# Delta-rule norms by a product with ones, a logarithm and an exponential, in place of column sums, roots and broadcasts

## What is computed

```python
def l2norm(x):
    return x * lax.rsqrt(jnp.sum(x * x, axis=-1, keepdims=True) + EPS)

q = l2norm(q.reshape(B, T, DN_HEADS, DN_DK)) * (DN_DK ** -0.5)
k = l2norm(k.reshape(B, T, DN_HEADS, DN_DK))
...
o, S = gated_delta_rule(q, k, v, g, beta, S0.astype(f32))
```

## Time and profile before

| | |
|---|---|
| median of 3 runs | 2141.03 us (2140.2 to 2142.7) |
| the profiled execution, its own time | 2148.23 us |
| its span | 2146.4 us |
| busy: TensorE (PE) | 1877.8 us, 87% |
| busy: VectorE (DVE) | 1489.8 us, 69% |
| busy: ScalarE (ACT) | 853.6 us, 40% |
| busy: GpSimd (POOL) | 641.1 us, 30% |
| granted TensorE clock, mean | 0.952 |

### The profile page before, as it was taken

The page is one execution under the profiler, slowest core; times in us unless marked ns, Lnnn a source line. Parts: engine busy times, 40 slices in busy tenths (PEclk is TensorE's granted clock), DMA queues, the critical chain, the costliest instruction groups (busy, mean ns, idle before and its releaser), DMA issues.

```text
span 2146.4 us, 23913 instructions
## 1 busy us (share of the span) xinstructions
PE 1877.8 (87%) x7974; PEld 1222.9 (57%) x7974; DVE 1489.8 (69%) x3280; ACT 853.6 (40%) x2349; POOL 641.1 (30%) x549
## 2 busy tenths in 40 slices
PE   8999999899987899998799678899998877777776
PEld 7888998656655567776566345664454423322321
DVE  4063631388878678789887677888878667667664
ACT  2533111253523476457534135345523333333332
POOL 0000000124422433323334232344434444444432
PEclk9899999899999999999899889999998999999999
DMA  6243234799999999999789999899999999999997
GB/s 228 93 152 128 98 99 169 288 339 356 377 417 399 415 380 387 398 376 368 287 290 362 419 417 352 323 360 393 387 414 418 421 402 421 421 421 422 422 382 302
DMA packets 128564, 724.62 MB, mean 338 GB/s; under 512 B 16384, under 2 KB 23168, under 8 KB 58304
## 3 DMA queue, kind: packets, MB, share of 16 engines
q0 software_dynamic: 78336, 570.46, 66.7%
q1 hardware_dynamic: 49488, 150.49, 19.1%
q10 hardware_dynamic: 624, 2.23, 0.3%
HBM read 714.08 MB, written 8.52 MB: 337 GB/s over the span
## 4 chain that ended last, share of the span: by engine, by line
PE 54%; DMA 23%; DVE 14%; ACT 6%; issue 2%; POOL 1%; DVEq 0%; SPq 0%; POOLq 0%; ACTq 0%
DMA arena<-in_uv,arena 16%; PE ps L1061 13%; PE ps L1009 12%; PE ps L731 6%; DVE arena L1931 6%; PE ps L787 5%; PE ps L927 4%; DMA arena<-in_stream 3%; PE ps L878 2%; PE ps L951 2%; PE ps L868 2%; PE ps L877 2%; DMA arena<-in_w_a 2%; DMA arena<-in_w_out 2%; ACT arena L1456 1%
## 5 line engine op out<-in xcount | busy, mean ns | idle before, releaser
L1495 POOL DMA_INDIRECT arena<-in_uv,arena x544 | 640.0, 1176 | 1201.8 <-PE ps L1061 764.2
L1061 PE MATMUL ps<-arena 128*128 128x512 f32 (+1 forms) x1624 | 787.5, 622 | 119.5 <-ACT arena L1456 119.3
L1931 DVE CUSTOM_DVE_ANT_0 arena<-arena 128x1024 f32<-128x1024 f32 x544 | 659.9, 1220 | 260.4 <-DMA arena<-in_uv,arena 258.4
L1061 PEld LDWEIGHTS ps<-arena 128*128 128x128 f32 (+1 forms) x1624 | 288.4, 191 | 484.6 <-issue 283.1
L1470 ACT ACTIVATE gelu_d<-dots 128x2 f32<-128x2 f32 x272 | 55.4, 204 | 812.4 <-DVE dots L1931 811.6
L1009 PE MATMUL ps<-arena 128*128 128x294 f32 (+1 forms) x1152 | 292.8, 415 | 17.5 <-DMA arena<-in_stream 9.4
L1009 PEld LDWEIGHTS ps<-arena 128*128 128x128 f32 x1152 | 220.4, 192 | 91.4 <-issue 13.5
L927 PEld LDWEIGHTS ps<-arena 128*128 128x128 f32 x1024 | 134.7, 204 | 35.8 <-issue 14.3
L927 PE MATMUL ps<-arena 128*128 128x128 f32 (+1 forms) x1024 | 138.5, 296 | 17.8 <-DMA arena<-in_w_a 13.3
L731 PE MATMUL ps<-arena 128*128 128x256 f32 x640 | 144.1, 389 | 3.5 <-DVE arena L1518 3.0
L731 PEld LDWEIGHTS ps<-arena 128*128 128x128 f32 x640 | 124.8, 196 | 22.1 <-issue 3.4
(11 more groups left out here) (277 smaller groups left out, 2047.2 us busy)
## 6 DMA issues: line engine op xcount, KB each, us to landing
arena<-in_stream SPq DMA_DIRECT2D x144, 512.0 KB
arena<-in_w_a SPq DMA_DIRECT2D x32, 512.0 KB
arena<-in_w_out SPq DMA_DIRECT2D x32, 512.0 KB
arena<-in_w_q SPq DMA_DIRECT2D x32, 512.0 KB
arena<-in_uv,arena POOLq DMA_INDIRECT x544
spill<-arena SPq DMA_DIRECT2D x48, 80.0 KB
arena<-spill SPq DMA_DIRECT2D x2, 1920.0 KB, 15.5
arena<-in_x_t SPq DMA_DIRECT2D x8, 272.0 KB, 4.8
```

What stands on the lines that cost most here:

```text
L1061: mm = pe.matmul(ps[0:L, half, :], diag[on_pe(k) % NDIAG][:, 0:L], ring[k % SLOTS][:, D + half * 512:D + (half + 1) * 512], start=False, s ...
L1495: pool.indirect_dma_start(out=ring[kk % SLOTS], out_offset=None, in_=a["uv"], in_offset=bass.IndirectOffsetOnAxis(ap=idx[:, kk:kk + 1], ax ...
L1931: ins = dve.tensor_tensor_reduce(ring[s][:, 0:D], ring[s][:, 0:D], n2p if t == NTILE else n2[t % 2], 1.0, 0.0, ALU.mult, ALU.add, dots[k / ...
```

## The change

The squares are summed by a product with a 128x128 matrix of ones, whose result stands on all partitions at once, so nothing has to be spread. TensorE makes one product of 128x512 for q at stage b + 1, and one for k at stage b + 4. At stage b + 5 ScalarE takes the logarithm of each into `sq_q` and `sq_k` (which lie side by side, `both`), and one exponential over both with scale -0.5. VectorE's norm at stage b + 5 reads SBUF and waits for that exponential. The root at b + 2, the reciprocal at b + 3 and the tile `rqk` are gone.

```diff
@@ pe, delta
                 yield b + 1
                 pe.wait_ge(d_sq, nth(t, g))
-                for j, src in enumerate((sq_q, sq_k)):
-                    for i in range(HG):
-                        c = j * HG + i
-                        mm = pe.matmul(ps[0:L, 2 + 3 * g + PC, c:c + 1], src[:, hs.start + i, 0:L], ones[:, 0:1],
-                                       start=True, stop=True)
-                mm.then_inc(d_ssq, 1)
+                pe.matmul(bank(PC, P)[:, :, 0:L], ones[:, :], sq_q[:, hs, 0:L], start=True, stop=True).then_inc(d_ssq, 1)
 
                 yield b + 4
-                pe.wait_ge(d_rcp, nth(t, g))
-                for i in range(HG):
-                    pe.matmul(bank(PC, P)[:, i, 0:L], rqk[0:L, g, i:i + 1].broadcast_to([L, P]), ident[0:L, 0:L],
-                              start=True, stop=True)
                 pe.wait_ge(d_exp, nth(t, g))
-                for i in range(HG):
-                    mm = pe.matmul(bank(PA, P)[:, i, 0:L], rqk[0:L, g, HG + i:HG + i + 1].broadcast_to([L, P]),
-                                   ident[0:L, 0:L], start=True, stop=True)
-                mm.then_inc(d_rbc, 1)
+                pe.matmul(bank(PA, P)[:, :, 0:L], ones[:, :], sq_k[:, hs, 0:L], start=True, stop=True).then_inc(d_rbc, 1)
@@ act, delta
-                yield b + 2
-                act.wait_ge(d_ssq, nth(t, g))
-                act.activation(rqk[0:L, g, :], ps[0:L, 2 + 3 * g + PC, 0:2 * HG], ACT.Sqrt, bias=eps_col[0:L, 0:1]
-                               ).then_inc(d_root, 1)
-
                 yield b + 3
                 act.wait_ge(d_rel, nth(t, g))
                 act.activation(dec[0:L, hs, 0:L], dec[0:L, hs, 0:L], ACT.Exp, scale=-1.0)
                 act.activation(gam[:, hs, 0:L], bank(PA, P)[:, :, 0:L], ACT.Exp).then_inc(d_exp, 1)
+
+                yield b + 5
+                act.wait_ge(d_ssq, nth(t, g))
+                act.activation(sq_q[:, hs, 0:L], bank(PC, P)[:, :, 0:L], ACT.Ln, bias=eps_col[:, 0:1])
+                act.wait_ge(d_rbc, nth(t, g))
+                act.activation(sq_k[:, hs, 0:L], bank(PA, P)[:, :, 0:L], ACT.Ln, bias=eps_col[:, 0:1]
+                               ).then_inc(d_root, 1)
+                act.wait_ge(d_root, nth(t, g))
+                both = view(4 * D, 2, H, P)[:, :, hs, 0:L]
+                act.activation(both, both, ACT.Exp, scale=-0.5).then_inc(d_rcp, 1)
@@ dve, delta
-                yield b + 3
-                dve.wait_ge(d_root, nth(t, g))
-                dve.reciprocal(rqk[0:L, g, :], rqk[0:L, g, :]).then_inc(d_rcp, 1)
-
                 yield b + 5
-                dve.wait_ge(d_rbc, nth(t, g))
+                dve.wait_ge(d_rcp, nth(t, g))
                 dve.scalar_tensor_tensor(out=q[:, hs, :], in0=q[:, hs, :], scalar=float(P) ** -0.5,
-                                         in1=bank(PC, P)[:, :, 0:L], op0=ALU.mult, op1=ALU.mult)
-                dve.tensor_tensor(k[:, hs, :], k[:, hs, :], bank(PA, P)[:, :, 0:L], ALU.mult).then_inc(d_norm, 1)
+                                         in1=sq_q[:, hs, 0:L], op0=ALU.mult, op1=ALU.mult)
+                dve.tensor_tensor(k[:, hs, :], k[:, hs, :], sq_k[:, hs, 0:L], ALU.mult).then_inc(d_norm, 1)
```

More of the change, by code:

```diff
@@ L140, in trunk_program @@
         o_sb, o_sq = nmat, pmat
-        rqk = sb("rqk", [P, 2, H])
         keys0 = sb("keys0", [P, NKEYS])
```

## The result

The changed kernel takes 2165.22 us (median of 6 runs, 2156.01 to 2169.49) beside 2140.18 for the kernel before (2136.87 to 2142.70, 6 runs): a ratio of 1.0106, 95% interval 1.0089 to 1.0124, or +22.7 us (19.1 to 26.5). The profiled execution of the changed kernel took 2167.55 us, with a span of 2165.7. The forecast was 2155, in a range of 2140 to 2166; the forecast case itself ended at 2162.

The account below looks back on a forecast made before the run. No one engine was taken to bound the kernel: TensorE at tile 0, waits between engines at tiles 1 and 2, DMA at tile 4. Terms -3.1 + 3.5 + 8.1 + 3.5 + 2 = +14 us gave 2155 us, range 2140 to 2166.

Parts of the forecast that it names:

- the forecast case: Whole kernel: the summed walk over tiles 0 to 4, 2155 us, lying between 2147 and 2162; chance 0.67.
- Tile 0, -3.1: Tile 0, where TensorE is full: 3.5 us of relief gained almost whole, 0.4 left for ScalarE's longer chain; -3.1 us.
- The block, 4.7 us: ScalarE, one group's norm: load 1.28, two logarithms 1.1, load 1.28, exponential 1.05; 4.7 us in one piece.
- The loads, four more: ScalarE's table loads rise by four: tile 1 one more, tile 2 three, tile 3 one fewer, tile 4 one more.
- Tile 1, +3.5: Tile 1: norm g1 ends at 453.5 instead of 450.06, behind ScalarE's two blocks; +3.5 us.
- Tile 2, +8.1: Tile 2: norm g1 ends at 1056.4 instead of 1048.26, all passed on; +8.1 us, the largest term.
- Tile 3, +3.5: Tile 3: norm g1 ends at 1325.4 instead of 1321.9; +3.5 us.
- Tile 4, +2: Tile 4: a 7 us stall, mostly covered by gathers in flight with DMA at 0.99; +2 us, from 0 to 7.
- One table serves both functions: Rival, ScalarE: one table set has logarithm and exponential, so each block loses its second load; +6.9, 2148 us, chance 0.06.
- The ring takes the stalls up: Rival: rows already fetched let VectorE make up nearly all after each tile; -3 to +4, 2141 us, chance 0.14.
- TensorE's relief decides: Rival: TensorE's backlog sets the stretches, so its relief counts in all tiles; -19, 2122 us, chance 0.05.
- More is lost: The fourth rival: no stall caught up, lower clock after each, tile 4 in full; +26, 2167 us, chance 0.08.

Follow-up runs that it names:

- e12: Kernel before with the new form at tiles 1 to 4, tile 0 left as before: 2167.22 us, ratio 1.0113 to the kernel before.
- e9: The changed kernel measured once more, nothing else altered: 2162.22 us, ratio 1.0089 to the kernel before.
- e10: Kernel before with the new form at tile 1 alone: 2147.56 us, ratio 1.0019.
- e2: Kernel before with the new form at tile 2 alone: 2148.74 us, ratio 1.0031.
- e11: Kernel before with the new form at tile 3 alone: 2143.04 us, ratio 1.0012.
- e3: Kernel before with the new form at tile 4 alone: 2148.65 us, ratio 1.0031.
- e1: Kernel before with the new form at tile 0 alone: 2138.71 us, ratio 0.9992.
- e5: Changed kernel with both groups' logarithms, then both groups' exponentials, joined in one block a tile: 2162.32 us, ratio 1.0084 to the kernel before.
- e8: Kernel before with both groups' roots in one stage and both groups' exponentials in the next: 2148.13 us, ratio 1.0018.
- e4: Changed kernel with Identity for the logarithms and Square for the exponential over q and k, norms not computed: 2146.15 us, ratio 1.0024 to the kernel before.

## Why the prediction came out as it did

The direction and the cause were as forecast, the size fell short: +14 us where +19 to +23 were measured. The result lies above the forecast case, which ended at 2162, and is inside the range only because that was drawn up to the fourth rival. By its own steps:

- **Tile 0, -3.1.** The traces give -4.8 (one execution of three at -6.7, the others at -3.6 and -4.0), e12 against e9 -5.0. The products take what was costed: 0.86 us each at full clock. Confirmed, a little small.
- **The block, 4.7 us.** Measured 4.95. The logarithm out of PSUM takes 0.69 and not the exponential's 0.58 (a bias column was not in the row that it was taken from); the exponential 1.06 and the loads 1.28 are as taken from the earlier trace rows.
- **The loads, four more.** 202 before, 206 after: ten at the logarithm, ten at its exponential. Confirmed, and tile by tile: e10, e2, e11 and e3, with the change at tile 1, 2, 3 and 4 alone, have 203, 205, 201 and 203, as the order of the stages had given it (one more, three, one fewer, one more).
- **Tile 1, +3.5.** Stage +5.5, timed alone +4.1 (0.4 to 7.9). The wait of about 7 us for g0 was forecast and is 7.06. From dot 2 to dot 8 the changed form takes 5.7 to 7.5 us more than before's trace (changed, e9, e10, e12), the old form in e1, e2, e3 and e11 0.0 to 1.8 more; the means lie 5.7 apart. The walk took dot 5 from before's trace, where it starts 13.9 us behind the tile's head (431.72 less 417.8); in the changed kernel it starts 16.0 behind it (423.06 less 407.1), since dot 4 waited 2.22 us for its gather and not 0.17, and all that follows is late by as much. Before's dot 5 is the earliest of the nine traces (the others have 16.0 to 18.3, in either form). In the old form a dot 5 at 16.2 costs nothing yet (e3), since ScalarE gets through the root's load and to the Gelu only 17.4 us behind the head (435.23 in before); in the new form that load is gone and the Gelu waits for the dot. The walk let it start at 15.2, it started at 17.2 (424.33). The term was 2 us short, by a dot that the walk had held fixed.
- **Tile 2, +8.1.** Like against like 6.3 to 7.8 in the long way, 9.1 in the short; stage +11.0; timed alone +6.6. Confirmed in size. Whether it is the largest term is open: tile 4 costs about as much.
- **Tile 3, +3.5.** Stage +3.9, dots 242 to 248 +4.2, timed alone +2.6. Confirmed in the traces, in the medians alone undecided.
- **Tile 4, +2: the step that failed.** The stall was worked out at 7 us, and then "the gathers in flight cover a stall of that length, and VectorE can catch up. I count +2". Up to dot 296 the dots show 7.8 us in the changed kernel, 8.0 in e12 and 7.8 in e9, e3 alone 8.1 and +6.6 in time. Rows in flight gave back some 2 us of it by dot 304, and by dot 320 the loss was 7.6 again (e3 above). A high DMA share had been read as cover. What the trace shows is that the gathers stall with VectorE: in the window around tile 4 the DMA share falls from 0.99 to 0.83 and GpSimd's busy time from 19.96 to 14.71 us. A ring slot is freed when its row has been added, which comes behind its dot, so a stop of the dots stops the gathers too, and where DMA was the full engine its lost time was not made up. With 7.8 in place of 2 the forecast's sum is +19.8.

**The rivals.** *One table serves both functions* is out: ten loads ahead of the logarithms and ten ahead of the exponentials behind them, 1.28 us each. The Trainium skill's rule (ScalarE: Activation LUTs, Table sets), by which a logarithm followed by an exponential needs one load, is not borne out by this kernel as it was built. Nor is the drain of some 1380 ns that the same page adds to each load (What ACT_TABLE_LOAD costs): each function starts 0.01 us after its load, and each load 0.01 to 0.02 us after the function ahead of it. *The ring takes the stalls up* is out for tiles 2 and 4 (e2, e3), and for tile 1 by the dots (from dot 2 to dot 160 the new form is still 5.2 us longer), where e10's timed runs come near its 1 us. *TensorE's relief decides* held at tile 0 alone. *More is lost*, 2167 us, comes nearer to the measured 2165.2 and 2162.2 than the forecast's own 2155, and for its tile 4 it had the right size. What of its +26 goes to the lower clock it didn't say. That half is seen at two tiles: the granted clock of the window is 0.76 where it was 0.87 at tile 2, and 0.87 where it was 0.96 at tile 4, while at tile 1 it stays at 0.93. At tile 2, after 5.60 us of idling, a product takes 2.07 in the changed kernel where it takes 1.13 in e9; what that costs in the end was not separated.

**What stays open.** Why e5 loses 18 us, in spite of the relief at tile 0, with 13 us of added waits at these lines. Its trace gives a place for some of the rest: from dot 290 to dot 320 it takes 84.7 us, as long as the changed kernel, though its waits at these lines are shorter there, and over all it has VectorE wait 69.5 us for TensorE behind the first dot, against 58.3 before; no run separates this. Open too is which condition sends tile 2 the one way or the other.

## What to carry to other kernels

Price a stall by who waits behind it and not by the number of table loads: 13 loads fewer gained nothing (e8), while the loads in the block that VectorE stood before made three quarters of the loss (e4). Where DMA was nearly full (0.99) and the consumer freed the slots, the rows in flight did not cover the consumer's stall: they gave back 2 of 8 us, and two dozen dots later nearly the whole stall stood in the time again. If a change helps at one tile and hurts at others, build it tile by tile: here the new form pays at tile 0, where TensorE is full, and nowhere else, and even the form that pays there is worth about a quarter of a per cent by the traces.

## What the runs showed of the hardware

- In this kernel as built, two logarithms and an exponential over them come with a load each way, 1283 ns, every time (x10 and x10).
- The logarithm of 128x512 out of PSUM with a column as bias takes 0.69 us (mean 688 ns), the exponential out of PSUM without one 0.58 (mean 591). With a function in place of the logarithm that needed no load (Identity, e4) the same row takes 676 ns.
- The execution before the first tile's deltas ends at one of a few moments: the head of tile 0 comes at 190.9 to 191.6 us in six traces, at 193.8 and 194.4 in two and at 196.6 to 197.0 in six, whatever was changed behind it. These 6 us and the 5 us between the two ways of tile 2 are of the size of the 12 us by which single runs of one kernel lie off its median.
